# A hybrid encoder layer: V split ahead of the softmax, the next pair's queries ahead of a weight chunk, and a bias table stored straight from SBUF

## What is computed

```python
h = layer_norm(x, ln_in_g, ln_in_b)                  # x: 512 x 2048
proj = h @ w_in                                      # 14608 columns, split in twelve
# A: sliding-window attention, 16 heads of 64, with a relative bias from rel_table
# B: forgetting attention, 16 heads of 64, causal:
sc = einsum('bqhd,bkhd->bhqk', qb, k) * HD_B ** -0.5
sc = sc + cq[..., :, None] - cum_logf[:, :, None, :]  # then the causal mask
p = jax.nn.softmax(sc, axis=-1)
ob = einsum('bhqk,bkhd->bqhd', p, v)
# C: cross-attention, 4 heads of 256, into 256 memory tokens
branches = (oa * silu(ag), ob * silu(bg), oc * silu(cg))
merged = sum(sigmoid(mg_n + b_gate_n) * (branches[n] @ w_branch[n]) for n in range(3))
h = layer_norm(alpha * h + merged @ w_out, ln_g, ln_b)
```

## Time and profile before

| | |
|---|---|
| median of 3 runs | 1900.26 us (1899.64 to 1901.17) |
| the profiled execution | 1899.64 us, span 1898.1 us |
| TensorE, VectorE, ScalarE busy | 97%, 69%, 45% of the span |
| branch C | about 125 to 350 us |
| branch B | about 520 to 777 us, a pass in 31.2 us |
| mean granted TensorE clock | 0.989 of 2.4 GHz |

### The profile page before, as it was taken

How to read it: one execution, slowest core, us unless ns; L and a number is a source line. 1 busy time by engine, 2 the same in 40 slices (tenths; PEclk the granted TensorE clock), 3 DMA queues, 4 the chain that set the end, 5 groups by cost and what they waited for, 6 DMA issues and landing times.

```text
span 1898.1 us, 24011 instructions
## 1 busy us (share of the span) xinstructions
PE 1838.4 (97%) x8503; PEld 1514.7 (80%) x8503; DVE 1304.1 (69%) x2063; ACT 855.8 (45%) x1440; POOL 206.8 (11%) x279
## 2 busy tenths in 40 slices
PE   8999779999999999999999999999999999999995
PEld 6888567788878888888888888888888888888884
DVE  5774655578767676566668878778788645576776
ACT  4652222345455555344445455455456333234543
POOL 1112111100111111000000000000001000003223
PEclk9999899999999999999999999999999999999998
DMA  8587665963643433333334614615336644439998
GB/s 307 191 200 188 160 167 145 301 154 131 185 140 110 127 84 95 92 93 101 88 104 150 222 58 164 209 35 200 126 141 235 208 153 148 145 116 240 241 209 190
DMA packets 227413, 301.48 MB, mean 159 GB/s; under 512 B 13632, under 2 KB 140672, under 8 KB 225152
## 3 DMA queue, kind: packets, MB, share of 16 engines
q1 hardware_dynamic: 171824, 188.24, 31.3%
q0 software_dynamic: 55360, 111.61, 22.3%
q10 hardware_dynamic: 144, 0.52, 0.1%
HBM read 247.73 MB, written 50.97 MB: 157 GB/s over the span
## 4 chain that ended last, share of the span: by engine, by line
PE 86%; DMA 4%; DVE 3%; ACT 3%; issue 2%; POOL 1%; DVEq 0%; ACTq 0%; POOLq 0%; SPq 0%
PE acc L659 8%; PE acc L661 8%; PE acc L660 7%; PE scores L838 6%; PE scores L842 6%; PE scores L840 6%; PE acc L842 3%; PE acc L840 3%; PE acc L838 3%; PE transposed L684 3%; PE scores L1081 2%; PE scores L1079 2%; PE scores L1080 2%; PE attended L842 2%; PE attended L840 2%
## 5 line engine op out<-in xcount | busy, mean ns | idle before, releaser
L1263 ACT ACTIVATE piece_split<-w 128x512 fp32r<-128x512 f32 x448 | 282.5, 632 | 292.6 <-PE scores L842 109.1
L1793 DVE TENSOR_TENSOR piece_split<-w,piece_split 128x512 fp32r<-128x512 f32 x448 | 308.9, 691 | 113.7 <-ACT piece_split L1263 101.3
L1652 DVE TENSOR_TENSOR w_lo<-raw_weights,w_hi 128x1024 fp32r<-128x1024 f32 x182 | 221.6, 1220 | 185.1 <-ACT w_hi L1162 182.7
L659 PE MATMUL acc<-h_hi,w_lo 128*128 128x512 f32 x800 | 323.0, 404 | 0.0
L661 PE MATMUL acc<-h_hi,w_hi 128*128 128x512 f32 x800 | 313.8, 392 | 0.0
L660 PE MATMUL acc<-h_lo,w_hi 128*128 128x512 f32 x800 | 312.9, 391 | 0.0
L1162 ACT ACTIVATE w_hi<-raw_weights 128x1024 fp32r<-128x1024 f32 x182 | 191.7, 1057 | 204.4 <-PE acc L1081 52.1
L659 PEld LDWEIGHTS acc<-h_hi,w_lo 128*128 128x128 f32 x800 | 152.1, 190 | 31.5 <-issue 2.8
L661 PEld LDWEIGHTS acc<-h_hi,w_hi 128*128 128x128 f32 x800 | 151.0, 189 | 32.8
L660 PEld LDWEIGHTS acc<-h_lo,w_hi 128*128 128x128 f32 x800 | 151.7, 190 | 30.1 <-issue 1.0
L838 PE MATMUL scores<-piece_split,h_lo 128*128 128x512 f32 x384 | 149.6, 390 | 0.0
(11 more groups left out here) (421 smaller groups left out, 3630.3 us busy)
## 6 DMA issues: line engine op xcount, KB each, us to landing
w<-in_w_in SPq DMA_DIRECT2D x128, 512.0 KB, 8.0
raw_weights<-in_w_in SPq DMA_DIRECT2D x102, 512.0 KB, 3.8
raw_weights<-in_w_branch SPq DMA_DIRECT2D x48, 512.0 KB, 5.2
raw_weights<-in_w_mem_kv SPq DMA_DIRECT2D x32, 512.0 KB, 5.6
gate<-gate_scratch POOLq DMA_DIRECT2D x12, 1024.0 KB, 6.7
h_sums<-sums_scratch POOLq DMA_DIRECT2D x6, 1024.0 KB, 11.6
gate_scratch<-first_product POOLq DMA_DIRECT2D x12, 512.0 KB, 6.7
out_w_x<-in_w_out POOLq DMA_DIRECT2D x12, 512.0 KB, 8.4
```

The costliest lines, as they stand in the source:

```text
L659: pe.matmul(bank_out, wl, hi[:, k, :], start=first, stop=False)
L1263: act.activation(p_split[:, n % RING, 0, :], sources[p][:, k, :], ACT.Copy).then_inc(pc_hi, 1)
L1652: dve.tensor_tensor(w_lo[:, slot, :], raw[:, slot, :], w_hi[:, slot, :].bitcast(F32), ALU.subtract).then_inc(lo_ready, 1)
L1793: dve.tensor_tensor(p_split[:, n % RING, 1, :], sources[p][:, k, :], p_split[:, n % RING, 0, :].bitcast(F32), ALU.subtract).then_inc(pc_lo, 1)
```

## The change

Four things are changed.

- The V split moves to the head of step 1 on ScalarE and on VectorE. On VectorE it stands before the first head's maximum, and the first normalisation goes behind the chunk's split.
- At step 2 the next queries' high parts go ahead of the chunk's split on ScalarE, and on VectorE the second normalisation goes behind it.
- POOL waits for `gated` and stores `b_sum` before it loads V.
- The intermediate `toep_rows` goes, and with it its store and the wait. The 128-fold copies read `toep_sb` in SBUF, two pairs in each of the four heads. The waits for `toep_stored` count 16 less.

```diff
@@ ScalarE, gate_group
-                                act.wait_ge(toep_stored, 16 + 16 * PAIRS)
+                                act.wait_ge(toep_stored, 16 * PAIRS)
@@ ScalarE, b_pass
                     if s == 1:
+                        act.wait_ge(v_loaded, 32 + 32 * i)
+                        act.activation(b_v[:, :, :, 0, :], b_v_raw[:, :, :, 1, :], ACT.Copy).then_inc(b_v_hi, 1)
                         b_exps(0)
                     if s == 2:
                         b_probs_hi(0, (0, 1, 2, 3))
                         if not last_pair:
                             k_hi(2 + i)
                         b_exps(1)
+                        if not last_pair:
+                            q_hi(CH_P + 1, 4, i, acc[JOB_P % 2])
                     split_hi(CH_P + s, 4, i)
-                    if s == 1:
-                        act.wait_ge(v_loaded, 32 + 32 * i)
-                        act.activation(b_v[:, :, :, 0, :], b_v_raw[:, :, :, 1, :], ACT.Copy).then_inc(b_v_hi, 1)
-                    if s == 2 and not last_pair:
-                        q_hi(CH_P + 1, 4, i, acc[JOB_P % 2])
@@ VectorE, b_pass
                     if s == 1:
+                        dve.wait_ge(b_v_hi, 1 + i)
+                        dve.tensor_tensor(b_v[:, :, :, 1, :], b_v_raw[:, :, :, 1, :],
+                                          b_v[:, :, :, 0, :].bitcast(F32), ALU.subtract).then_inc(v_ready, 1)
                         b_max(0)
-                        b_normalise(0)
                     if s == 2:
                         b_probs_lo(0, (0, 1))
                         b_max(1)
                         b_probs_lo(0, (2, 3))
                         if not last_pair:
                             k_lo(2 + i)
-                        b_normalise(1)
                     split_lo(CH_P + s, 4, i)
                     if s == 1:
-                        dve.wait_ge(b_v_hi, 1 + i)
-                        dve.tensor_tensor(b_v[:, :, :, 1, :], b_v_raw[:, :, :, 1, :],
-                                          b_v[:, :, :, 0, :].bitcast(F32), ALU.subtract).then_inc(v_ready, 1)
+                        b_normalise(0)
                     if s == 2:
+                        b_normalise(1)
                         if last_pair:
                             a_keys()
@@ POOL, branch C
                     pool.wait_ge(toep_copied, 1)
-                    pool.dma_start(toep_rows, toep_sb[:, :]).then_inc(toep_stored, 16)
-                    pool.wait_ge(toep_stored, 16)
-                for n in range(3 * i, min(3 * i + 3, PAIRS)):
+                for n in (2 * i, 2 * i + 1):
                     pair = slice(2 * n, 2 * n + 2)
-                    pool.dma_start(toep.ap()[pair], toep_rows[pair].unsqueeze(1).broadcast_to((2, P, TOEP)))\
+                    pool.dma_start(toep.ap()[pair], toep_sb[pair, :].unsqueeze(1).broadcast_to((2, P, TOEP)))\
                         .then_inc(toep_stored, 16)
@@ POOL, branch B
                 if i:
+                    pool.wait_ge(gated, BT + i)
+                    pool.dma_start(br_dram[1, i - 1], b_sum[:, :]).then_inc(br_stored, 16)
                     pool.wait_ge(b_o, 2 * i)
                     load_v(i)
-                    pool.wait_ge(gated, BT + i)
-                    pool.dma_start(br_dram[1, i - 1], b_sum[:, :]).then_inc(br_stored, 16)
```

More of the change, by code:

```diff
@@ L179, in program @@
     kv_dram = nc.dram_tensor("keys_values_scratch", (2, TT, P, BW), F32, kind="Internal").ap()
-    toep_rows = nc.dram_tensor("toeplitz_rows_scratch", (HEADS, TOEP), F32, kind="Internal").ap()
     toep = nc.dram_tensor("toeplitz_scratch", (HEADS, P, TOEP), F32, kind="Internal")
@@ L2648, in _ @@
             pool.dma_start(br_dram[1, PAIRS - 1], b_sum[:, :]).then_inc(br_stored, 16)
-            pool.wait_ge(toep_stored, 16 + 16 * PAIRS)
+            pool.wait_ge(toep_stored, 16 * PAIRS)
             pool.wait_ge(k_ready, PAIRS + 1)
```

## The result

The changed kernel takes 2022.5 us (median of 4 runs, 2020.5 to 2024.3) against 1900.4: the ratio is 1.064, with a 95% interval of 1.062 to 1.066. It is 122 us slower, 54 us beyond the forecast of 1969 us and 37 us beyond the upper end of the range. The profiled execution has a span of 2017.8 us, 119.7 us more than before.

What follows compares the result with a forecast made beforehand. TensorE, busy 97% of the span, was taken to bound the kernel, so its stalls cost in full. The profiled 1899.6 us plus 62.5 for branch B and 7 for the table copies gave 1969 us, range 1940 to 1986.

Steps and rivals of the forecast that it cites:

- part 3: Branch C: table copies straight from SBUF take 20 us and delay two sum-tile stores, 7 us together.
- parts 1 and 2: Branch B: V loaded later, split before first softmax (1); queries and weight chunk before second normalisation (2); together 62.5 us.
- the first wait: Branch B, first head's transposes: TensorE waits for probabilities held up by late V, 4.0 us in seven passes.
- the second wait: Branch B, second head's transposes: TensorE waits for the later normalisation, 2.1 us a pass.
- the third wait: Branch B, after the second head's first transposes: TensorE's present 0.47 us wait for VectorE's copies grows by 0.8 us.
- the clock: Branch B: TensorE's clock falls after stalls, costing 1.5 us for the 4.0 us stall and 0.4 us for the later pair.
- the other two heads have room, head 0 the least: Branch C: copies in the other two heads delay nothing; at most 2 us more from head 0, left to the range.
- (a): Rival, branch C: copies from SBUF are as quick as from DRAM, -0.5 us there, 1962 us in all; chance 0.25.
- (b): Rival, branch B: TensorE's clock holds because in-between work is dense, 1956 us; chance 0.12.
- (c): Rival, branch B: V lands in time, so only the second head's reordering costs, 1924 to 1931 us; chance 0.06.
- (d): Rival, branch B: clock low through most of a pass, 1.7 us more in seven passes, 1980 to 1990 us; chance 0.14.
- (e): Rival, branch C: not slower, since DMA relief brings norm rows sooner, 1897 us; chance 0.03, including 0.01 no change.

Runs made afterwards that it cites:

- e1: Kernel before with only the bias table copied straight from SBUF, two neighbouring pairs a head, no DRAM bounce: 1952.0 us, ratio 1.028, +52.7 us.
- e2: Kernel before with all of the change except the bias-table copies, so only branch B's reorderings: 1968.3 us, ratio 1.037, +69.0 us.
- after: The changed kernel with all of the change, against the kernel before: 2022.5 us, ratio 1.064, +122 us.
- e5: Kernel before with V split ahead of the first softmax, first normalisation behind the weight part, and V loaded behind the gated output: 1949.9 us, ratio 1.026.
- e7: Kernel before with next queries ahead of the weight chunk on ScalarE and second normalisation behind it on VectorE: 1923.7 us, ratio 1.012.
- e10: Kernel before with only the next queries' high parts moved ahead of the weight part on ScalarE, VectorE's order unchanged: 1921.3 us, ratio 1.011.
- e6: Kernel before with V split and first normalisation moved on ScalarE and VectorE, but POOL unchanged, so V is loaded early: 1900.4 us, ratio 1.000.
- e4: Kernel before with the table copies spread as two pairs a head in place of three, still from DRAM: 1899.5 us, ratio 1.000.
- e9: Kernel before with the next head's norm rows loaded in branch C as soon as the buffer is free: 1884.7 us, ratio 0.992.
- e12: Kernel before with e9's early norm rows and the eight table copies, still from DRAM, moved from branch C to B: 1872.2 us, ratio 0.985.
- e8: Kernel before with only POOL's order changed, V loaded behind the gated output, both splits left where they were: 1899.0 us, ratio 0.999.
- e11: Kernel before with only the second normalisation moved behind the weight's low part on VectorE, ScalarE's order unchanged: 1905.2 us, ratio 1.003.

## Why the prediction was wrong

| term | forecast | measured |
|---|---|---|
| part 3 | 7 us | 52.7 us (e1) |
| parts 1 and 2, branch B | 62.5 us | 69.0 us (e2); B is 67.4 us longer in e2 and in after |
| of it the first wait | 4.0 us, seven times, 28.0 | 34.3 us in after, 34.7 in e5: 4.9 to 5.0 each |
| the second wait | 2.1 us a pass, 15.6 | 13.2 us in after, 13.3 in e7 |
| the third wait grows | 5.6 us | after: 9.0 - 3.3 = 5.7; e2 and e7: by none |
| the clock | 1.9 us a pass, 13.3 | after: 67.4 - 47.5 - 5.7 = 14.2 us; e2: 67.4 - 47.0 = 20.4 us |

**The step that failed is part 3's.** It said that only two stores wait behind the copies, that the copies take 20 us and each store 2.6 us more for its bytes on four engines, and that "the other two heads have room, head 0 the least". Three things in it were off, and the runs show each.

The first is head 0. The copies hold back not only what POOL queues behind them. The load that ScalarE waits for there goes by SP's queue, and it took 26.9 us. The traffic of head 1 shows what such a load waits for: between 206 and 210 SP's queue moved 780 of the 1040 packets of the load issued at 206, just three quarters, and the load landed only 30.8 us after its issue, some 4 us after the last copy. That its last quarter sat on the four engines of 16 that the copies held fits this; no view shows a single engine. The prediction looked at POOL's ring alone and never asked what SP's loads do while four engines are held for 20 us. That is head 0's share of TensorE's waits, 12.9 us (13.4 in e1), which I had put at 2 us at most. The prediction's last sentence names this case: "if the copies hold up something that I take to have room".

The second is the length. Counted from the landing of the norm's rows, which go ahead of them in POOL's queue, to the landing of the second copy, the pair took not 20 us but 29.6 in head 1 (203.0 to 232.6), 28.6 in head 2, and 30.6 in head 0, where no rows go ahead, from its issue. The 37.6 us in head 1 are the same length and some 8 us in the queue behind these rows. Of the 10 us too few, 4 are the rate: the 8.2 GB/s for an engine that I took from a small transfer gave 33 GB/s, the windows have 27, and 655 KB take 24 us at that. With the rate alone put right the sum would have been 15 us. The other 5 to 6 us are open; in head 1 some fall between 203 and 206, where 9 GB/s were moved. The store of the tiles, issued meanwhile, landed 22.1 us after its issue, 5.0 us behind the copies where I had 3.0. VectorE's wait is 19.4 and 18.3 us against 3.57 and 2.90: +15.8 and +15.4, where I had +3.4 and +3.7. In head 1 the length makes 9.6 us of that difference and the landing behind it 2.0.

The third comes after branch C: 7.3 us in two waits of TensorE for the pieces of the next stage (`piece_split` in e1). ScalarE waits 14.58 us for a load of w there, and in the trace of after the first loads of w land 17.9 us after their issue while head 3's copies are still out. The sum had nothing there. The three make 13.4 + (25.9 + 24.8 - 19.6) + 7.3 = 51.8 of e1's 52.7 us.

**The mechanism in B was right, and one size was off.** V was taken to land 3.4 us after its issue, between V's own row and K's; in the new place its median is 4.8 us. The issue came as predicted (614.79 is E + 4.1; 592.11 was E + 4.2), and the chain from the start of the V part to the turned probabilities took 7.8 us (620.52 to 628.33; forecast 8.1). So the wait is 4.9 us and not 4.0: 6.3 us over the passes. The second wait was 1.9 us and not 2.1. The clock's 14.2 us are near the forecast's 13.3, but that is in part luck, for the terms within it were not right. In the changed kernel the clock falls once in each of the seven passes with a late V, and after none of the seven second waits, for which I had 0.4 us each; the fall that followed the 1.8 us wait at the start of B is gone too (the clock is 1.00 over 578 to 584). Within B, part 1 alone (e5) loses 49.5 - 34.7 = 14.8 us by the clock, part 2 alone (e7) 22.1 - 12.3 = 9.8 us, 1.4 a pass. In e2 the clock falls after both waits of a pass and costs 20.4 us, so B is as long as in after by another split. That is also what makes the third wait differ. TensorE in e2, where the line of after at 647.72 above has 1.15 us:

```profile
592.41 0.94 PE L684 MATMUL transposed<-ident,b_probs 128*128 128x128 f32 x3 [0.46 <-DVE b_probs_t_lo L2054]
```

Where the clock has fallen after the second wait, TensorE comes later to the third and waits 0.46 us; where it has not, it waits 1.15 us. This is the argument of the forecast (a slow TensorE arrives later at a wait that is there anyhow), and here it is borne out. Why the same wait of 1.9 us lowers the clock in e2 and e7 and not in after is open.

**The rivals.** (a), quick copies, is refuted by e1. (b), the clock holds, is refuted by e2 and e10. (c), V in time, is refuted by e5; for it to hold V would have to be loaded early, which is e6. (d), a low clock for most of a pass, did not happen in the whole change: 1.7 us more a pass would be 25 us of clock, after has 14.2; e2, with two falls a pass, has 20.4. (e), not slower by DMA relief, is refuted by e4: two pairs a head give nothing. The path to a faster kernel lay in the same rows, but in another edit: the rows of the norm and the place of the copies (e9, e12).

## What to carry to other kernels

Here a transfer that was slow on some four DMA engines delayed the loads of another queue too: before moving one, ask how long the engines are held and how deep each ring is, not only what stands behind it in its own queue. A source in few neighbouring partitions of SBUF is to be spread over distant ones (here still 3.8 us slower), or bounced through DRAM. Two moves that are each free can be dear together (e6 and e8 against e5), because both draw on the same room: add up what is taken out of the room between a producer's end and its reader's start. A wait of TensorE is to be priced with its clock: here a wait that grew from 0.5 to 1.1 us cost 0.8 us a pass (e11), and one that grew from 0.5 to 1.9 us cost 2.7 in B (e10). That price is not certain, since in the changed kernel waits of 1.9 us left the clock alone.

## What the runs showed of the hardware

- The same 128-fold copy moved 105 GB/s out of DRAM, 55 GB/s out of two groups of two partitions eight apart, and 27 GB/s out of four neighbours, each at a share of 0.26 of the 16 engines.
- A weight load of 512 KB on another queue landed 26.9 us after its issue while the copies held some four engines (15.7 us at 55 GB/s, 3.8 us before the change). A later one, of whose 1040 packets SP's queue had moved 780 within 4 us, took 30.8 us.
- A pair of copies out of four neighbours took 28.6 to 30.6 us (heads 0 to 2) for 655 KB, where 27 GB/s give 24; between 203 and 206 in head 1 the share was 0.11 and 9 GB/s were moved. The cause is open.
- TensorE's granted clock stayed at 1.00 through passes with a wait of 1.1 us (e11). Waits of 1.9 us were followed by a fall in seven cases of seven in e7, six of seven in e10, and none of seven in the changed kernel; the 1.8 us wait at the start of B by one before, and by none in after and e1.
